# Splitting the first weight unit in two halves and reordering the first loads and the angle sums of an encoder kernel

## The chip, the cores and the metric
The kernel runs on one core of a Trainium2 chip. The metric is the device time of one execution in microseconds (us). The kernel before took 1182.69 us (median of three runs, 1182.65 to 1182.70). The engines are called PE (TensorE, matrix products), DVE (VectorE), ACT (ScalarE), POOL (GpSimd) and SP (the sync queue, which only issues transfers). POOL issues transfers too.

## The reference: what is computed
Two layers of an encoder on 512 tokens of width 1024. Each layer normalises x, modulates it by shift and scale (rows of c_act @ w_ada), multiplies it by the input weights w_in, and so on:

```python
c_act = jax.nn.silu(c)
mod = c_act @ w_ada[l] + b_ada[l]
sh1, sc1, g1, sh2, sc2, g2 = jnp.split(mod, 6, axis=-1)
h = modulate(rms_norm(x, norm1_g[l]), sh1, sc1)
z = h @ w_in[l]
za, zb, zq, zk, zv = jnp.split(z, split_idx, axis=-1)
...   # conformer convolution, short gated convolution, differential attention
x = x + g1[:, None, :] * mix
h = modulate(rms_norm(x, norm2_g[l]), sh2, sc2)
x = x + g2[:, None, :] * swiglu(h, w_gate_up[l], w_down[l])
```

The attention turns its queries and keys by cosines and sines of angles, positions times inverse frequencies (rope). These angles don't depend on x and are needed only after the first products.

## The kernel before, in words
Tokens lie along the free dimension: x is xT, 8 chunks (k = 0 to 7) of 128 features by 512 tokens. Every float32 product is made of three products of split operands (hi times hi, hi times lo, lo times hi). So each weight unit (a tile of 128 x 1024, 512 KB) lands in one of two `raw` slots, ACT copies it rounded into `w_hi` (`split_hi`, L676), and DVE subtracts to make `w_lo` (`split_lo`, L1108). SP loads unit u into slot u % 2 once `w_lo` of unit u - 2 is made (the loop at L512 to L515). `w_hi` and `w_lo` are rings of four.

**The first norm** is the place of the change. All of it is written out by hand, in program order on each engine:
- PE: three warm-up products, the spread of c over the partitions (L1916), 14 warm-up products of ones (`warm_up`, L1792, two records each in the trace), the sum of squares over the partitions (L1921, four products of 512 columns, two records each), 11 more warm-ups, and then for each chunk k an `a_chunk` (12 products, L1833, L1834, L1841: unit 0 for k = 0 and 1, unit 2 for k = 2 and 3, ...) and a `k_chunk` (12 products, L1851 to L1853: unit 1 for k = 0 and 1, unit 3 for k = 2 and 3, unit 5 for k = 4 and 5, unit 7 for 6 and 7). So 24 products stand for one chunk. An even chunk reads the first 512 columns of its unit and an odd chunk the second 512.
- ACT: silu of c, eight squares of x (L902), a table load, `split_hi(0)`, then rstd = exp(-0.5 ln(...)) in two steps (L745, L747) once the sum of squares is there, and `first_gain(0)` (L753, L755: the shift and gain of chunk 0). For each chunk: `norm_hi` (h_hi, L765), `split_hi(k + 1)`, `first_gain(k + 1)`. Behind it in chunk 3 a table load, in chunk 4 the three sines and a table load.
- DVE: the angles in turns (`angle_turns`, `sum_angles`: L1142, L1143 and the reduction L1144), four pair sums of the squares (L1138), `mod_dot(0)`, `mod_dot(1)` (L1161), `split_lo(0)`. Then for each chunk k: `norm_apply` (L1184, to work_b), one `mod_dot`, `norm_lo` (h_lo, L1192), another `mod_dot`, `split_lo(k + 1)`. In chunk 0 the order is apply, h_lo, mod_dot(2), split_lo(1), mod_dot(3). `reduce_angles` (L1148 to L1153, five small operations) stands behind chunk 1.
- `mod_dot(m)` is the product of silu(c) with block m of w_ada (512 KB, `ada_ring_first`). Blocks 2k and 2k + 1 are shift and scale of chunk k. POOL loads all sixteen (L540): 0 and 1 once the second quarter of x is there, 2 and 3 as 0 and 1 land, and block m from 4 on once DVE has finished m - 3 of them.

SP issues c, positions, frequencies, the four quarters of x, pcol (small per-feature constants), unit 0, and unit 1 once modulation block 0 has landed.

## Time and profile before
| | |
|---|---|
| median of three runs | 1182.69 us |
| the profiled execution | 1182.13 us, of which the span is 1180.3 us |
| PE busy | 99% of the span |
| DVE, ACT, POOL busy | 61%, 44%, 11% |

The span is what the profiler records from the first to the last instruction; 1.83 us of the execution lie around it. The times in rows are microseconds from the span's start. In a row of the timeline the columns are start, length, engine, line, operation, tiles, shapes, the count of merged records, and in brackets the engine's idle time before it with what ended it.

### The profile page before, as it was taken

To read this page: it belongs to the slowest core of one execution; us is meant where nothing else is said; L and a number is where in the kernel's file an instruction comes from. 1 tells how busy PE (TensorE), PEld (TensorE's weight loads), DVE (VectorE), ACT (ScalarE), POOL (GpSimd) and SP (SyncE) were. 2 spreads that over 40 slices of the span, in tenths; PEclk is the share of its full clock that TensorE was granted. 3 is DMA by queue.
4 is the path that set the end of the run, shared out by engine and by line. 5 is a ranking of instruction groups with operands and counts; after the bars stand their busy time and mean duration, and the time that the engine had idled before them with its cause. 6 is when DMAs were issued, how large, how long until landed. Compare 5 with 4: busy or idle time off the path is not lost.

```text
span 1180.3 us, 14480 instructions
## 1 busy us (share of the span) xinstructions
PE 1169.5 (99%) x5168; PEld 933.3 (79%) x5168; DVE 718.1 (61%) x1028; ACT 515.7 (44%) x782; POOL 125.0 (11%) x207
## 2 busy tenths in 40 slices
PE   9999999999999999999999999999999999999998
PEld 6787656878888888888888877578888888888887
DVE  7989888985555433577478988757633332333231
ACT  5576787452232323322234468866432222332220
POOL 2323233210102000121000112100000000000000
PEclk9999999999999999999999999999999999999999
DMA  8679477885655222697223663422322323233222
GB/s 307 246 179 252 79 188 227 301 277 191 198 192 178 89 96 99 233 323 252 101 91 104 162 143 72 108 71 91 124 90 93 102 89 107 89 104 101 102 105 87
DMA packets 50668, 178.32 MB, mean 151 GB/s; under 512 B 5889, under 2 KB 6017, under 8 KB 50626
## 3 DMA queue, kind: packets, MB, share of 16 engines
q1 hardware_dynamic: 30386, 107.13, 26.7%
q0 software_dynamic: 20240, 70.66, 21.8%
q8 instruction: 23, 0.38, 0.1%
q14 instruction: 19, 0.16, 0.0%
HBM read 172.52 MB, written 2.10 MB: 148 GB/s over the span
## 4 chain that ended last, share of the span: by engine, by line
PE 86%; DVE 8%; ACT 4%; issue 2%; DVEq 0%; ACTq 0%; POOL 0%; POOLq 0%
PE ps L1785 22%; PE ps L1786 22%; PE ps L1787 22%; PE ps L1814 3%; DVE uc L1296 2%; PE ps L1851 2%; PE ps L1853 2%; PE ps L1852 2%; PE ps L1818 2%; PE ps L2056 1%; PE ps L1908 1%; ACT prob L815 1%; PE ps L2031 1%; PE ps L1841 1%; PE ps L1833 1%
## 5 line engine op out<-in xcount | busy, mean ns | idle before, releaser
L676 ACT ACTIVATE w_hi<-raw 128x1024 fp32r<-128x1024 f32 x196 | 207.4, 1059 | 514.5 <-PE ps L1787 466.5
L1108 DVE TENSOR_TENSOR w_lo<-raw,w_hi 128x1024 fp32r<-128x1024 f32 x164 | 201.2, 1227 | 240.3 <-ACT w_hi L676 238.1
L1785 PE MATMUL ps<-h_hi,w_hi 128*128 128x512 f32 x832 | 331.5, 398 | 0.0
L1787 PE MATMUL ps<-h_lo,w_hi 128*128 128x512 f32 x832 | 324.2, 390 | 0.0
L1786 PE MATMUL ps<-h_hi,w_lo 128*128 128x512 f32 x832 | 324.1, 390 | 0.0
L1785 PEld LDWEIGHTS ps<-h_hi,w_hi 128*128 128x128 f32 x832 | 156.2, 188 | 43.4 <-issue 12.2
L1786 PEld LDWEIGHTS ps<-h_hi,w_lo 128*128 128x128 f32 x832 | 156.3, 188 | 34.0 <-issue 2.9
L1787 PEld LDWEIGHTS ps<-h_lo,w_hi 128*128 128x128 f32 x832 | 156.2, 188 | 32.7
L1786 PE MATMUL ps<-gu_hi,w_lo 128*128 128x512 f32 x352 | 137.0, 389 | 0.0
L1787 PE MATMUL ps<-gu_lo,w_hi 128*128 128x512 f32 x352 | 137.0, 389 | 0.0
L1785 PE MATMUL ps<-gu_hi,w_hi 128*128 128x512 f32 x352 | 137.0, 389 | 0.0
L1692 DVE TENSOR_TENSOR work_b<-ps,work_a 128x512 f32<-128x512 f32 x42 | 29.0, 691 | 110.0 <-PE ps L1787 86.6
L1787 PEld LDWEIGHTS ps<-gu_lo,w_hi 128*128 128x128 f32 x352 | 66.1, 188 | 13.7
L1785 PEld LDWEIGHTS ps<-gu_hi,w_hi 128*128 128x128 f32 x352 | 66.1, 188 | 13.7
L1786 PEld LDWEIGHTS ps<-gu_hi,w_lo 128*128 128x128 f32 x352 | 66.1, 188 | 13.7
L1851 PE MATMUL ps<-w_hi,h_hi 128*128 128x512 f32 x192 | 75.2, 392 | 0.2 <-DVE w_lo L1108 0.2
L1853 PE MATMUL ps<-w_hi,h_lo 128*128 128x512 f32 x192 | 74.8, 389 | 0.0
L1852 PE MATMUL ps<-w_lo,h_hi 128*128 128x512 f32 x192 | 74.8, 389 | 0.0
L1296 DVE SCALAR_TENSOR_TENSOR uc<-ua,pcol,uc 128x512 f32<-128x512 f32 x106 | 72.8, 743 | 0.0
L815 ACT ACTIVATE prob<-ps,neg_max 128x512 f32<-128x512 f32 x64 | 43.2, 682 | 16.8 <-DVE neg_max L1408 16.7
L1469 DVE SCALAR_TENSOR_TENSOR xT<-ps,mod,xT 128x512 f32<-128x512 f32 x31 | 23.2, 747 | 40.6 <-PE ps L1787 38.4
L1408 DVE TENSOR_REDUCE neg_max<-ps 128x2 f32<-128x1024 f32 x32 | 39.0, 1219 | 12.5 <-PE ps L2031 7.0
(229 smaller groups left out, 1408.6 us busy)
## 6 DMA issues: line engine op xcount, KB each, us to landing
raw<-w_stream SPq DMA_DIRECT2D x196, 512.0 KB, 3.3
w_lo<-w_stream POOLq DMA_DIRECT2D x32, 512.0 KB, 7.9
ada_ring_gu<-ada POOLq DMA_DIRECT2D x28, 512.0 KB, 4.2
ada_ring_late<-ada POOLq DMA_DIRECT2D x28, 512.0 KB, 5.4
ada_ring_first<-ada POOLq DMA_DIRECT2D x16, 512.0 KB, 5.0
ada_ring_mid_a<-ada POOLq DMA_DIRECT2D x12, 512.0 KB, 5.1
ada_ring_mid_b<-ada POOLq DMA_DIRECT2D x12, 512.0 KB, 6.0
tap_sum<-tap_product POOLq DMA_DIRECT2D x12, 256.0 KB, 7.2
```

The costliest lines, as they stand in the source:

```text
L676: act.activation(w_hi[:, u % RING, :], raw[:, u % RAW, :], ACT.Copy).then_inc(s_whi, 1)
L815: act.activation(prob[:, it % PROBS, comp, :], ps[:, 2 * (it % 2) + comp, :], ACT.Exp, bias=neg_max[:, it, comp:comp + 1], accum_out=row_s ...
L1108: dve.tensor_tensor(w_lo[:, u % RING, :], raw[:, u % RAW, :], w_hi[:, u % RING, :].bitcast(F32), ALU.subtract).then_inc(s_wlo, 1)
L1296: dve.scalar_tensor_tensor(uc[:, c, :], ua[:, c, j:j + T], w, uc[:, c, :], ALU.mult, ALU.add).then_inc(s_tap, 1)
L1408: dve.tensor_reduce(neg_max[:, it, :], ps[:, b:b + 2, :], AX_X, ALU.max, negate=True).then_inc(s_max, 1)
L1785: pe.matmul(dst, whi, rhs[0][:, n, :], start=start, stop=False)
L1786: pe.matmul(dst, wlo, rhs[0][:, n, :], start=False, stop=False)
L1787: return pe.matmul(dst, whi, rhs[1][:, n, :], start=False, stop=stop)
L1814: pe.matmul(ps[:, bank, :], wp[:, u % RING, n * P:(n + 1) * P], rhs[0][:, n, :], start=b == 0 and wp is w_hi, stop=False)
L1851: pe.matmul(ps[:, bank, :], hs[0], ws[0], start=n == 0, stop=False)
L1852: pe.matmul(ps[:, bank, :], hs[0], ws[1], start=False, stop=False)
L1853: return pe.matmul(ps[:, bank, :], hs[1], ws[0], start=False, stop=n == KC - 1)
```

## The change
It does the following, all in the first norm of the first layer:
- The sum of the angles (the reduction over nine terms) moves on DVE from ahead of the pair sums to behind chunk 3, `reduce_angles` from behind chunk 1 to behind chunk 4; on ACT the table load and the sines move one chunk later.
- Weight unit 0 lands, is copied and is subtracted in two halves of 512 columns. The first half's copy on ACT stands behind rstd instead of ahead of it; the second half's stands in chunk 0, and so does its subtraction on DVE, behind mod_dot(3).
- SP issues modulation blocks 1, 0, 2 and 3 in place of POOL; DVE takes block 1 before block 0. SP's loop over later units begins once the second half of unit 0 has its `w_lo`.
- PE has 9 warm-ups instead of 14 ahead of the sum of squares, and 18 instead of 11 behind it; its chunk 1 waits for the second half of unit 0.

```diff
@@ semaphores @@
+        s_rawpart = sem("second_half_first_unit_landed")
+        s_whipart = sem("second_half_first_unit_hi")
+        s_wlopart = sem("second_half_first_unit_lo")
+        s_adafirst = [sem(f"ada_first_landed{i}") for i in range(4)]
...
@@ sync queue @@
-            for j in range(RAW):
-                if j == 1:
-                    ada_landed(sp, 0)
-                sp.dma_start(raw[:, j, :], w_in[j]).then_inc(s_raw[j], 16)
+            sp.wait_ge(s_x[0], 16)
+            for m in (1, 0):
+                sp.dma_start(ada_slot(m), ada_in[m]).then_inc(s_adafirst[m], 16)
+            sp.dma_start(raw[:, 0, 0:T], w_in[0][:, 0:T]).then_inc(s_raw[0], 16)
+            ada_landed(sp, 1)
+            sp.dma_start(raw[:, 1, :], w_in[1]).then_inc(s_raw[1], 16)
+            sp.dma_start(ada_slot(2), ada_in[2]).then_inc(s_adafirst[2], 16)
+            sp.dma_start(raw[:, 0, T:UE], w_in[0][:, T:UE]).then_inc(s_rawpart, 16)
+            sp.dma_start(ada_slot(3), ada_in[3]).then_inc(s_adafirst[3], 16)
+            sp.wait_ge(s_wlopart, 1)
             begin = RAW
@@ GpSimd queue @@
-            pool.wait_ge(s_x[KC // 2 - 3], 16)
-            for m in range(2):
-                ada_load(m)
-            for m in range(2, 4):
+            for m in range(4, 6):
                 ada_landed(pool, m - 2)
                 ada_load(m)
-            for m in range(4, M_MID):
+            for m in range(6, M_MID):
                 pool.wait_ge(s_acc, m - 4 + 1)
                 ada_load(m)
@@ scalar engine @@
-            split_hi(0)
             norm_rstd(0)
+            act.wait_ge(s_raw[0], 16)
+            act.activation(w_hi[:, 0, 0:T], raw[:, 0, 0:T], ACT.Copy).then_inc(s_whi, 1)
             act.wait_ge(s_pc, 16)
...
+                        if k == 0:
+                            act.wait_ge(s_rawpart, 16)
+                            act.activation(w_hi[:, 0, T:UE], raw[:, 0, T:UE], ACT.Copy).then_inc(s_whipart, 1)
                         if k + 1 < KC:
                             first_gain(k + 1)
-                        if k == 3:
+                        if k == 4:
                             act.preload_act_table_set("silu_and_others")
-                        if k == 4:
+                        if k == 5:
                             act.wait_ge(s_ang, N_ANGLE)
@@ vector engine @@
-            def sum_angles():
+            def whole_turns():
 
                 done(dve.tensor_scalar(whole[:], turns[:], ROUND, None, ALU.add))
                 done(dve.scalar_tensor_tensor(turns[:], whole[:], ROUND, turns[:], ALU.subtract, ALU.subtract))
+
+            def sum_angles():
+
                 done(dve.tensor_reduce(ang[:, 0], turns[:], AX_X, ALU.add))
...
             angle_turns()
-            sum_angles()
+            whole_turns()
...
+            mod_dot(1)
             mod_dot(0)
-            mod_dot(1)
-            split_lo(0)
+            dve.wait_ge(s_whi, 1)
+            dve.tensor_tensor(w_lo[:, 0, 0:T], raw[:, 0, 0:T], w_hi[:, 0, 0:T].bitcast(F32),
+                              ALU.subtract).then_inc(s_wlo, 1)
...
+                        if k == 0:
+                            dve.wait_ge(s_whipart, 1)
+                            dve.tensor_tensor(w_lo[:, 0, T:UE], raw[:, 0, T:UE], w_hi[:, 0, T:UE].bitcast(F32),
+                                              ALU.subtract).then_inc(s_wlopart, 1)
                         if k:
                             split_lo(k + 1)
-                        if k == 1:
+                        if k == 3:
+                            sum_angles()
+                        if k == 4:
                             reduce_angles()
@@ tensor engine @@
                 weights_split(u)
+                if u == 0 and r:
+                    pe.wait_ge(s_wlopart, 1)
...
-            warm_up(N_WARM)
+            warm_up(N_WARM - 5)
...
-            warm_up(N_WARM - 3)
+            warm_up(N_WARM + 4)
```

DVE around the first chunk, before (L1144 is the angle reduction, L1138 the pair sums, L1161 the mod_dots, L1184 and L1192 the two operations of a norm chunk):

```order
L1144 TENSOR_REDUCE ang<-turns 128x128
L1138 TENSOR_TENSOR sq_first<-sq_first 128x512 x4
L1486 SCALAR_TENSOR_TENSOR n_biased<-pcol 128x8
L1161 SCALAR_TENSOR_TENSOR ada_ring_first,mod_raw<-ada_ring_first,c_b 128x1024 x2
L1108 TENSOR_TENSOR w_lo<-raw,w_hi 128x1024
L1184 SCALAR_TENSOR_TENSOR work_b<-xT,gain,rstd 128x512
L1192 SCALAR_TENSOR_TENSOR h_lo<-work_b,mod,h_hi 128x512
L1161 SCALAR_TENSOR_TENSOR ada_ring_first,mod_raw<-ada_ring_first,c_b 128x1024
L1108 TENSOR_TENSOR w_lo<-raw,w_hi 128x1024
L1161 SCALAR_TENSOR_TENSOR ada_ring_first,mod_raw<-ada_ring_first,c_b 128x1024
L1184 SCALAR_TENSOR_TENSOR work_b<-xT,gain,rstd 128x512
L1161 SCALAR_TENSOR_TENSOR ada_ring_first,mod_raw<-ada_ring_first,c_b 128x1024
```

and now (there the mod_dots are L1178, norm_apply L1201, norm_lo L1209, a whole `split_lo` L1122):

```order
L1152 TENSOR_TENSOR sq_first<-sq_first 128x512 x4
L1503 SCALAR_TENSOR_TENSOR n_biased<-pcol 128x8
L1178 SCALAR_TENSOR_TENSOR ada_ring_first,mod_raw<-ada_ring_first,c_b 128x1024 x2
L1509 TENSOR_TENSOR w_lo<-raw,w_hi 128x512
L1201 SCALAR_TENSOR_TENSOR work_b<-xT,gain,rstd 128x512
L1209 SCALAR_TENSOR_TENSOR h_lo<-work_b,mod,h_hi 128x512
L1178 SCALAR_TENSOR_TENSOR ada_ring_first,mod_raw<-ada_ring_first,c_b 128x1024
L1122 TENSOR_TENSOR w_lo<-raw,w_hi 128x1024
L1178 SCALAR_TENSOR_TENSOR ada_ring_first,mod_raw<-ada_ring_first,c_b 128x1024
L1529 TENSOR_TENSOR w_lo<-raw,w_hi 128x512
L1201 SCALAR_TENSOR_TENSOR work_b<-xT,gain,rstd 128x512
L1178 SCALAR_TENSOR_TENSOR ada_ring_first,mod_raw<-ada_ring_first,c_b 128x1024
```

The reduction has gone from ahead of the pair sums, `w_lo` of unit 0 is two operations of 512 columns, and the second of them stands between mod_dot(3) and the `norm_apply` of chunk 1.

SP from the quarters of x on, before, with what each waits for:

```order
L500 DMA xT<-x_t 128x1024 x4
L501 DMA pcol<-pcol 128x278
L505 DMA raw<-w_stream 128x1024
L505 DMA raw<-w_stream 128x1024 [waits ada_landed0]
L512 UNCONDITIONAL_BRANCH
L512 ISA
L515 ISA [waits weight_lo]
L515 DMA raw<-w_stream 128x1024
```

and now:

```order
L507 DMA xT<-x_t 128x1024 x4
L508 DMA pcol<-pcol 128x278
L511 DMA ada_ring_first<-ada 128x1024 [waits x_landed0]
L511 DMA ada_ring_first<-ada 128x1024
L512 DMA raw<-w_stream 128x512
L514 DMA raw<-w_stream 128x1024 [waits ada_first_landed1]
L515 DMA ada_ring_first<-ada 128x1024
L516 DMA raw<-w_stream 128x512
L517 DMA ada_ring_first<-ada 128x1024
L525 UNCONDITIONAL_BRANCH [waits second_half_first_unit_lo]
L525 ISA
L528 ISA [waits weight_lo]
L528 DMA raw<-w_stream 128x1024
```

Three modulation blocks and the halves of unit 0 have come in around unit 1 (`raw` 128x1024 at L514), a fourth block behind them, and the load of unit 2 (the first in the loop, L528) stands behind a wait for the second half's `w_lo`.

PE up to its first product of the layer, before and now:

```order
L1916 MATMUL ps<-c_row,ones 128x512 x2
L1792 MATMUL ps<-ones 128x128 x14
L1921 MATMUL ps<-sq_first,ones 128x512 x4
L1792 MATMUL ps<-ones 128x128 x11
L1833 MATMUL ps<-h_hi,w_hi 128x512
```

```order
L1943 MATMUL ps<-c_row,ones 128x512 x2
L1817 MATMUL ps<-ones 128x128 x9
L1948 MATMUL ps<-sq_first,ones 128x512 x4
L1817 MATMUL ps<-ones 128x128 x18
L1860 MATMUL ps<-h_hi,w_hi 128x512
```

The sum of squares stands five products earlier, and as many products and two more stand behind it.

## Rows read from the trace of the kernel before

**Rows 1.** The page, busy time by engine
```profile
PE 1169.5 (99%) x5168; PEld 933.3 (79%) x5168; DVE 718.1 (61%) x1028; ACT 515.7 (44%) x782; POOL 125.0 (11%) x207
```

**Rows 2.** Waits, 0 to 35 us: who for whom, us in total, times, longest
```profile
PE ps L1833 <- ACT h_hi L765: 2.0, 3, 1.2
```

**Rows 3.** Waits of PE, 35 to 110 us
```profile
PE ps L1851 <- DVE w_lo L1108: 0.2, 1, 0.2
```

**Rows 4.** Timeline of PE
```profile
6.35 6.10 PE L1792 MATMUL ps<-ones 128*128 128x128 f32 x28
12.29 3.60 PE L1921 MATMUL ps<-sq_first,ones 128*128 128x512 f32 x8
15.72 2.62 PE L1792 MATMUL ps<-ones 128*128 128x128 f32 x22
...
19.50 0.47 PE L1833 MATMUL ps<-h_hi,w_hi 128*128 128x512 f32 x1 [1.16 <-ACT h_hi L765]
...
35.29 0.50 PE L1851 MATMUL ps<-w_hi,h_hi 128*128 128x512 f32 x1 [0.24 <-DVE w_lo L1108]
...
46.32 0.39 PE L1851 MATMUL ps<-w_hi,h_hi 128*128 128x512 f32 x1
```

**Rows 5.** Timeline of DVE
```profile
9.41 1.35 DVE L1144 TENSOR_REDUCE ang<-turns 128x128 f32<-128x1152 f32 x1
10.80 2.50 DVE L1138 TENSOR_TENSOR sq_first<-sq_first 128x512 f32<-128x512 f32 x4
...
14.86 1.23 DVE L1161 SCALAR_TENSOR_TENSOR ada_ring_first<-ada_ring_first,c_b 128x1024 f32<-128x1024 f32 x1
...
16.01 1.22 DVE L1108 TENSOR_TENSOR w_lo<-raw,w_hi 128x1024 fp32r<-128x1024 f32 x1
17.85 0.75 DVE L1184 SCALAR_TENSOR_TENSOR work_b<-xT,gain,rstd 128x512 f32<-128x512 f32 x1 [0.62 <-ACT gain L755]
19.39 0.75 DVE L1192 SCALAR_TENSOR_TENSOR h_lo<-work_b,mod,h_hi 128x512 fp32r<-128x512 f32 x1 [0.79 <-ACT h_hi L765]
...
24.21 0.75 DVE L1184 SCALAR_TENSOR_TENSOR work_b<-xT,gain,rstd 128x512 f32<-128x512 f32 x1 [0.64 <-ACT gain L755]
...
28.96 0.22 DVE L1148 TENSOR_SCALAR ang<-ang 128x128 f32<-128x128 f32 x1
...
30.39 0.75 DVE L1184 SCALAR_TENSOR_TENSOR work_b<-xT,gain,rstd 128x512 f32<-128x512 f32 x1
...
34.02 1.22 DVE L1108 TENSOR_TENSOR w_lo<-raw,w_hi 128x1024 fp32r<-128x1024 f32 x1
35.15 0.74 DVE L1184 SCALAR_TENSOR_TENSOR work_b<-xT,gain,rstd 128x512 f32<-128x512 f32 x1
...
44.66 0.74 DVE L1184 SCALAR_TENSOR_TENSOR work_b<-xT,gain,rstd 128x512 f32<-128x512 f32 x1
```

**Rows 6.** Timeline of ACT
```profile
7.38 4.44 ACT L902 ACTIVATE sq_first<-xT 128x512 f32<-128x512 f32 x8
...
13.13 1.06 ACT L676 ACTIVATE w_hi<-raw 128x1024 fp32r<-128x1024 f32 x1
15.93 0.69 ACT L745 ACTIVATE rstd<-ps,eps 128x512 f32<-128x512 f32 x1 [1.74 <-PE ps L1921]
...
17.18 0.28 ACT L753 ACTIVATE mod<-mod_raw,pcol 128x1 f32<-128x1 f32 x1
...
43.64 0.30 ACT L753 ACTIVATE mod<-mod_raw,pcol 128x1 f32<-128x1 f32 x1 [1.19 <-DVE ada_ring_first L1161]
...
46.13 0.73 ACT L765 ACTIVATE h_hi<-work_b,mod 128x512 fp32r<-128x512 f32 x1
```

**Rows 7.** Tile raw, issue of unit 1 at 13.6 us: issue to landing
```profile
DMA to landing us min/median/max: 3.4/3.4/3.4
```

**Rows 8.** Tile raw, issue of unit 3 at 22.6 us: issue to landing
```profile
DMA to landing us min/median/max: 4.7/4.7/4.7
```

**Rows 9.** Tile raw, issue of unit 2 at 17.4 us: issue to landing
```profile
DMA to landing us min/median/max: 7.4/7.4/7.4
```

More of the change, by code:

```diff
@@ L478, in ada_landed @@
                 eng.wait_ge(s_ada_gu[m % 4], 16 * ((m - M_GU) // 4 + 1))
+            elif m < 4:
+                eng.wait_ge(s_adafirst[m], 16)
             else:
                 before = m // 8 if m < M_GU else M_GU // 8 + (m - M_DOWN) // 8
-                eng.wait_ge(s_ada[m % 8 if m < M_GU else (m - M_DOWN) % 8], 16 * (before + 1))
+                slot = m % 8 if m < M_GU else (m - M_DOWN) % 8
+                eng.wait_ge(s_ada[slot], 16 * (before + (slot >= 4)))
         def chunks_before(k):
```

## The prediction
> **What bounds the kernel now.** I read the page first: PE is busy for 1169.5 of 1180.3 us [rows 1], so the time is PE's work plus the little that PE waits. The waits by engine say where: up to 35 us PE waits 2.0 us in three pieces for h_hi [rows 2], and from 35 to 110 us only once, 0.2 us [rows 3]. PE's timeline puts that last wait at 35.29 us, where chunk 2's k_chunk starts as `w_lo` of unit 3 is made [rows 4]. From there PE runs back to back: from 35.29 to 46.32 us are two chunks, 5.5 us each, where DVE needs 4.75 (35.15 to 44.66 for two) [rows 4, 5]. So whatever moves the k_chunk at 35.29 moves the end by as much, and what comes onto DVE behind it is paid by its slack, if that is enough.
>
> The point at 35.29 hangs on DVE: the `norm_apply` of chunk 2 starts at 30.39, and everything between (two mod_dots, h_lo, `w_lo` of unit 3 at 34.02) is dense, 4.90 us to PE's start [rows 4, 5]. I call that operation apply(2) and follow it. The profiled execution took 1182.13 us, 1.83 more than its span, 0.56 less than the median of 1182.69. I take a difference of spans as the difference of times and put it on the median.
>
> **The angle reduction ahead of the pairs.** It takes 1.35 us and sits right ahead of the pair sums [rows 5]. Without it the pairs can start at 9.42 instead of 10.80, but the squares come at 0.555 us each until 11.82 [rows 6], so the fourth pair starts at 11.85 and ends at about 12.5 (0.68 each), against 13.3 before. Some 0.8 of the 1.35 is gained.
>
> **The sum of squares on PE.** Before, 14 warm-ups (28 records, 6.10 us, 0.212 us a step) held PE till 12.29, then the sum took 3.43 us until 15.72 [rows 4]. Now nine warm-ups end at 6.35 + 18 x 0.212 = 10.2 us. But the trace shows the two clock levels: a step of a 128-column record is 0.212 us before 12.29 and 2.62 / 22 = 0.119 behind 15.72, and a record of the sum, four times as wide, takes 0.43, twice the early step only [rows 4]. So PE ran at 1.2 GHz up to about 12.2 us, although it had been at work since before 6.35, and at 2.4 GHz behind it. If the clock rises at the same moment now, 1.95 us of the sum run at half speed and do 0.97 of its 3.43 us. It ends at 12.2 + 2.45 = 14.65 us, 1.07 earlier. If the clock were up already, it would end at 10.25 + 3.43 = 13.7, 2.0 earlier. If it rose only after the sum, it would end at 10.25 + 6.86 = 17.1, 1.4 later. I take 14.65: the records of the sum are no less dense than the warm-ups whose place they take.
>
> **rstd, the first half and the first apply.** rstd started 0.21 behind the end of the sum and its two steps took 1.25 until 17.18 [rows 6], so now 14.86 to 16.1. In front of the gain stands the copy of the first half, half of the 1.06 us of the whole [rows 6], 0.55; before, the whole copy lay in ACT's wait for the sum at 13.13. Gain at 16.65 to 17.2. DVE's half subtraction (0.65, by 1.22 for the whole [rows 5]) runs beside the gain, 16.65 to 17.3. So apply(0) starts at 17.3 instead of 17.85: 0.55 earlier. The mod_dots are done by then: pairs to 12.7, two at 1.15 each [rows 5] make 15.0, if block 1 has landed by 12.7 and block 0 by 13.9. SP issues them once the first quarter of x is there, which ACT's first square shows to be by 7.38 [rows 6]; POOL had waited for the second quarter, and both blocks were used from 14.86 at the latest [rows 5]. 1.6 us of room lie behind 15.0 before they would count. PE's 18 warm-ups take 36 x 0.117 = 4.2 us and end at about 18.9; h_hi comes to PE 1.65 us behind apply(0) [rows 4, 5], at 18.95, so they cost at most 0.1 there.
>
> **Chunk 0 to 1.** From apply(0) on DVE does h_lo (1.54 later), mod_dot(2), `w_lo` of unit 1, mod_dot(3), and now the second half of unit 0: 17.3 + 1.54 + 0.67 + 3 x 1.14 = 22.93 is its start, 23.6 its end [rows 5]. It fills the wait of 0.64 us for the gain [rows 5], so apply(1) starts at 23.66 instead of 24.21, the same 0.55. PE's chunk 1 starts 1.65 behind that, past the half. Blocks 2 and 3, unit 1 and the second half are issued as block 1 lands, by my reckoning near 11.5 us, where unit 1 had been issued at 13.6 [rows 7], and are needed at 18.8 or later; I cost them at nothing.
>
> **Unit 2, the step that decides.** Its slot is free when all of unit 0 has been subtracted: before at 17.23, now at 23.6. It was issued at 17.4 and had landed at 24.8 [rows 9], in time for a copy that has to follow h_hi of chunk 1, 0.8 us behind 24.21 [rows 5]. Now it is issued at 23.8. How long does it fly? Unit 1 took 3.4 us into nearly empty queues [rows 7]; unit 3, issued at 22.6 with one block a microsecond ahead and one behind it, 4.7 [rows 8]; the longest is 7.4, with four blocks in flight ahead [rows 9]. At 23.8 block 7 is issued half a microsecond ahead and most of the earlier ones are down, between the first two, so I take 4.1: landed at 27.9. Copy 1.1 us, `w_lo` of unit 2 1.14 us, apply(2) at 27.9 + 0.05 + 1.1 + 1.14 = 30.2. Without this wait it would be at 24.21 - 0.55 + (30.39 - 24.21) - 1.43 = 28.4, since `reduce_angles` (28.96 to 30.39) has left [rows 5]. So of the 2.0 us won by then, 1.8 are given back: DVE waits for ACT, ACT for unit 2, and behind ACT's waiting copy stands the gain of chunk 2. apply(2) is 0.2 us early, with 3.4 in place of 4.1 it is 0.9 early, with 4.7 0.4 late. The Trainium skill, DMA: Bandwidth & Descriptors, "Anatomy of one DMA", gives a fixed 2.0 us plus the bytes at 436 GB/s; for 512 KB that is 3.2 us, an estimate by that page under which apply(2) would be 1.1 early. No landing here of a unit beside modulation blocks is so short [rows 8, 9].
>
> **Behind the point.** Relative to the k_chunk of chunk 2, DVE now has 1.37 (reduction) and 1.43 (`reduce_angles`) more. Its gain on PE is 0.7 us a chunk. Stepping through: unit 5's `w_lo` comes 0.16 before PE wants it, h_hi of chunk 5 0.1 late, h_hi of chunk 6 no later (ACT's gain to h_hi takes 2.49 with the sines between [rows 6], which now stand there), unit 7's `w_lo` another 0.2 late. I put 0.25 us for it, between 0 (PE ahead of nothing) and 0.6. Behind chunk 7 DVE has room and the angle tables are needed late.
>
> **Sum.** -0.2 + 0.25 = +0.05 us: 1182.69 + 0.05, no change, 1182.7 us.
>
> **The rivals.**
> (a) Unit 2 lands faster or the clock is up earlier. With 3.4 us in flight: -0.9 + 0.25 = -0.65. With the sum all at 2.4 GHz the whole start is 0.9 earlier: -1.1 at 4.1 us and -1.8 at 3.4, with 0.25 back -0.85 and -1.55. For it: the queues are emptier than at 22.6. Against: 0.212 us a step until 12.2 [rows 4]. Time 1181.6.
> (b) Slower: the sum of squares meets the low clock to its end. It decides if PE has not risen to 2.4 GHz by 17.1 us. Then rstd is 2.45 later than in my sum, nothing on DVE catches it up, and apply(2) is 2.25 late; with 0.25 behind it +2.5, 1185.2 us. For it: the five warm-ups taken away stood just where the clock rose. Against: the sum is as dense, and three runs before agree within 0.05 us, so the moment looks fixed. The Trainium skill, TensorE: Matmul & The Clock Gate, Part 1, says the moment depends on the run ("the same kernel measures 6, 11, or 14 cold-MMs"); by that the runs would scatter between (a) and (b). The trace does not agree so far.
> (c) Slower by the queue: unit 2 takes as long as it did before, 7.4 us, behind blocks 6 and 7. apply(2) is at 33.5, +3.1, with 0.25 +3.35: 1186.0 us.
> (d) Something of the 2.0 us kept that I give back (no wait for unit 2 at all): -2.0 + 0.25, 1180.9 us at most, with the high clock 1180.0.
>
> **How the numbers follow.** Forecast 0.50 (its own range 1182.0 to 1183.6), (a) 0.30, (b) 0.07, (c) 0.06, (d) 0.07. A difference under 0.2% (2.4 us) can't be told from no change in this kernel. Forecast, (a) and half of (d) lie inside it, (b) at its edge, (c) past it: faster 0.04, same 0.86, slower 0.10. The range for eight in ten holds the forecast and (a): 1181.1 to 1184.1.
>
> **What would show it.** Sum of squares ending at 14.6 to 14.7, its first two records twice as long as the last. apply(0) at 17.3, apply(1) at 23.7. SP's issue of unit 2 at 23.8 in place of 17.4, and ACT's copy of unit 2 idle for it for 2 to 3 us, which rows of before do not have. apply(2) near 30.2, k_chunk 2 near 35.1, and then short waits of PE for h_hi of chunk 5 and `w_lo` of unit 7. I am wrong if ACT has unit 2 at hand when it comes to it, if PE's sum ends past 16, or if PE idles more than half a microsecond behind 36 us.

## The result: 3.3 us slower, where no change was forecast
The changed kernel took 1185.6 us (median of nine runs, 1184.32 to 1187.29), the kernel before beside it 1182.33 (nine runs, 1181.59 to 1184.48). The ratio is 1.0027, its 95% interval 1.0018 to 1.0035: slower by 3.3 us, outside the forecast's range of 1181.1 to 1184.1. The ratios with their intervals are those on record; where a kernel has only five to nine runs they can differ from the quotient of the two medians by up to 0.0008, which is 0.9 us. The profiled execution took 1185.41 us with a span of 1183.6, 3.3 more than before's.

In this part lines are those of the changed kernel: 1817 is the warm-up, 1948 the sum of squares, 1860 the first product of an `a_chunk`, 1878 that of a `k_chunk`; on DVE 1201 is `norm_apply`, 1209 h_lo, 1178 mod_dot, 1122 `split_lo`, 1509 and 1529 the two halves of unit 0, 1161 the reduction; on ACT 686 is `split_hi`, 755 rstd, 775 h_hi, 917 the first half's copy.

The page's first row reads as it did [rows 1]: PE's share doesn't show 3 us, since waits of that size are 0.3% of the span.

```profile
PE 1170.7 (99%) x5172; PEld 932.4 (79%) x5172; DVE 718.8 (61%) x1029; ACT 515.6 (44%) x783; POOL 122.9 (10%) x203
```

PE's timeline of the changed kernel, against [rows 4]:

```profile
6.36 4.21 PE L1817 MATMUL ps<-ones 128*128 128x128 f32 x18
10.36 4.02 PE L1948 MATMUL ps<-sq_first,ones 128*128 128x512 f32 x8
14.22 4.18 PE L1817 MATMUL ps<-ones 128*128 128x128 f32 x36
18.64 0.47 PE L1860 MATMUL ps<-h_hi,w_hi 128*128 128x512 f32 x1 [0.24 <-ACT h_hi L775]
...
32.59 0.47 PE L1860 MATMUL ps<-h_hi,w_hi 128*128 128x512 f32 x1 [1.87 <-ACT h_hi L775]
...
35.84 0.50 PE L1878 MATMUL ps<-w_hi,h_hi 128*128 128x512 f32 x1 [0.24 <-DVE w_lo L1122]
...
58.91 0.50 PE L1878 MATMUL ps<-w_hi,h_hi 128*128 128x512 f32 x1 [0.81 <-DVE w_lo L1122]
...
101.12 0.50 PE L1878 MATMUL ps<-w_hi,h_hi 128*128 128x512 f32 x1 [0.87 <-DMA w_lo<-w_stream]
```

The start is as forecast: chunk 0 begins at 18.64 in place of 19.50. Then stand three waits that before has not, or has shorter: 1.87 us for h_hi of chunk 2, 0.81 for `w_lo` of unit 7, 0.87 for a weight unit near 100 us. DVE's and ACT's timelines say what the first one hangs on [rows 5, 6]; DVE's is this:

```profile
9.28 2.04 DVE L1152 TENSOR_TENSOR sq_first<-sq_first 128x512 f32<-128x512 f32 x3
...
16.38 0.69 DVE L1509 TENSOR_TENSOR w_lo<-raw,w_hi 128x512 fp32r<-128x512 f32 x1 [1.65 <-ACT w_hi L917]
16.99 0.75 DVE L1201 SCALAR_TENSOR_TENSOR work_b<-xT,gain,rstd 128x512 f32<-128x512 f32 x1
...
22.62 0.69 DVE L1529 TENSOR_TENSOR w_lo<-raw,w_hi 128x512 fp32r<-128x512 f32 x1
23.35 0.75 DVE L1201 SCALAR_TENSOR_TENSOR work_b<-xT,gain,rstd 128x512 f32<-128x512 f32 x1
...
29.81 1.23 DVE L1122 TENSOR_TENSOR w_lo<-raw,w_hi 128x1024 fp32r<-128x1024 f32 x1 [2.75 <-ACT w_hi L686]
30.95 0.74 DVE L1201 SCALAR_TENSOR_TENSOR work_b<-xT,gain,rstd 128x512 f32<-128x512 f32 x1
...
40.46 1.34 DVE L1161 TENSOR_REDUCE ang<-turns 128x128 f32<-128x1152 f32 x1
...
51.63 1.22 DVE L1122 TENSOR_TENSOR w_lo<-raw,w_hi 128x1024 fp32r<-128x1024 f32 x1
...
55.97 1.48 DVE L1178 SCALAR_TENSOR_TENSOR ada_ring_first<-ada_ring_first,c_b 128x1024 f32<-128x1024 f32 x1
...
57.38 1.47 DVE L1122 TENSOR_TENSOR w_lo<-raw,w_hi 128x1024 fp32r<-128x1024 f32 x1
```

ACT's, with its long wait for unit 2:

```profile
14.48 0.69 ACT L755 ACTIVATE rstd<-ps,eps 128x512 f32<-128x512 f32 x1 [1.54 <-PE ps L1948]
...
28.72 1.06 ACT L686 ACTIVATE w_hi<-raw 128x1024 fp32r<-128x1024 f32 x1 [3.85 <-DMA raw<-w_stream]
```

SP's timeline has the issue of units 2 and 3 (two transfers in one row), and the tile `raw` says for unit 2 how long it flew, in us from issue to landing, where [rows 9] had 7.4 for it, hidden:

```profile
23.66 0.89 SPq L528 DMA_DIRECT2D raw<-w_stream  x2
```

```profile
DMA to landing us min/median/max: 5.0/5.0/5.0
```

The chain reads: the second half of unit 0 is subtracted by 23.3, SP issues unit 2 at 23.66, it lands 5.0 us later, ACT copies at 28.72, DVE subtracts at 29.81 and applies chunk 2 at 30.95, which was at 30.39 before.

Three marks cut the difference into parts: the `k_chunk` of chunk 2, that of chunk 7, and the first transpose of k, in us from the span's start. Behind the last mark the rest of the span is 1074.0 to 1074.6 in all sixteen profiles, so all but a few tenths of a microsecond of the difference arises in the first 110 us.

| profile | k_chunk 2 | k_chunk 7 | transpose | span |
|---|---|---|---|---|
| before | 35.29 | 62.64 | 106.20 | 1180.3 |
| changed | 35.84 | 64.52 | 109.42 | 1183.6 |
| added in the part | +0.55 | +1.33 | +1.34 | +0.1 |

Up to the last mark that is 3.2 us, and 3.3 in the span.

### The profile page after: what moved, and what is told of

The parts are those of the page before. It is cut to its first block, busy times and chain, and to the rows that moved or that the text cites. A ratio compares the mean times of both kernels' runs of the same rounds, so it can differ in the third digit from the quotient of the medians.

```text
span 1183.6 us, 14491 instructions
## 1 busy us (share of the span) xinstructions
PE 1170.7 (99%) x5172; PEld 932.4 (79%) x5172; DVE 718.8 (61%) x1029; ACT 515.6 (44%) x783; POOL 122.9 (10%) x203
## 4 chain that ended last, share of the span: by engine, by line
PE 79%; DVE 8%; ACT 4%; DMA 2%; issue 2%; POOL 0%; DVEq 0%; ACTq 0%; SPq 0%; POOLq 0%
PE ps L1810 22%; PE ps L1812 22%; PE ps L1811 22%; PE ps L1839 3%; DVE uc L1313 2%; PE ps L1843 2%; PE ps L2083 1%; PE ps L1935 1%; ACT prob L825 1%; PE ps L2058 1%; DMA tap_sum<-tap_product 1%; DVE w_lo L1122 1%; PE ps L2071 1%; DMA w_lo<-w_stream 1%; PE ps L2052 1%
## 5 line engine op out<-in xcount | busy, mean ns | idle before, releaser
L1122 DVE TENSOR_TENSOR w_lo<-raw,w_hi 128x1024 fp32r<-128x1024 f32 x163 | 200.0, 1227 | 243.3 <-ACT w_hi L686 240.8
L1810 PEld LDWEIGHTS ps<-h_hi,w_hi 128*128 128x128 f32 x832 | 156.2, 188 | 43.2 <-issue 12.2
L1810 PEld LDWEIGHTS ps<-gu_hi,w_hi 128*128 128x128 f32 x352 | 66.1, 188 | 13.7
L1812 PEld LDWEIGHTS ps<-gu_lo,w_hi 128*128 128x128 f32 x352 | 66.1, 188 | 13.7
```

Source lines behind the costliest of these rows:

```text
L1122: dve.tensor_tensor(w_lo[:, u % RING, :], raw[:, u % RAW, :], w_hi[:, u % RING, :].bitcast(F32), ALU.subtract).then_inc(s_wlo, 1)
L1810: pe.matmul(dst, whi, rhs[0][:, n, :], start=start, stop=False)
L1812: return pe.matmul(dst, whi, rhs[1][:, n, :], start=False, stop=stop)
```

## The experiments
The theory from the two traces: (T) unit 2's late issue and its flight set chunk 2, and the angle work comes due at unit 7. The rivals: (R1) the angle move alone costs the time; (R2) the moved clock rise; (R3) the wait near 100 us is the change's doing.

**Which part costs.** The first is the kernel before with the angle moves alone.

```diff
-            sum_angles()
+            whole_turns()
@@ DVE, chunks (on ACT the table load and the sines move one chunk later too) @@
-                        if k == 1:
+                        if k == 3:
+                            sum_angles()
+                        if k == 4:
                             reduce_angles()
```

> The kernel before with only the angle sums moved (reduction behind chunk 3, reduce_angles behind chunk 4, table load and sines one chunk later on ACT). Theory 1 (the loss of the change comes from the late load of unit 2, and the angle work behind chunk 3 is mostly within DVE's slack): the k_chunk of chunk 2 starts 1.4 us earlier than before (33.9 us), 0.3 to 1.1 us are given back by short waits of PE in chunks 5 to 7, the time is 0.3 to 1.1 us below before. Rival (the moved angle work is what costs, since DVE has no room there): 0.5 us or more above before.

Measured: 1182.87 us against 1182.80, ratio 0.9999 (0.999 to 1.0008). R1 falls: it asked for 0.5 us or more above before. But the gain of 0.3 to 1.1 us that I expected isn't there either. The early part of it is, `k_chunk` 2 at 34.03, 1.3 us earlier than before, and it is given back in two waits, for unit 7 and for the unit near 100 us. PE's timeline of it:

```profile
56.62 0.50 PE L1856 MATMUL ps<-w_hi,h_hi 128*128 128x512 f32 x1 [0.57 <-DVE w_lo L1108]
...
98.59 0.50 PE L1856 MATMUL ps<-w_hi,h_hi 128*128 128x512 f32 x1 [0.75 <-DMA w_lo<-w_stream]
```

The second is the changed kernel with the angle work put back where it stood before.

```diff
             whole_turns()
+            sum_angles()
@@ DVE, chunks (on ACT the table load and the sines move back too) @@
-                        if k == 3:
-                            sum_angles()
-                        if k == 4:
+                        if k == 1:
                             reduce_angles()
```

> The changed kernel with the angle work back in its old places: only the loads, the halves and the warm-ups are changed. Theory 1: the pair sums are 1.3 us later again, unit 2 still lands late (near 29.3 us) and reduce_angles again stands between its w_lo and the norm_apply of chunk 2, so the k_chunk of chunk 2 starts near 38.0 us, 2.7 later than before; nothing is late behind it: 2.5 to 3.5 us above before. Rival (the angle work costs, the loads do not): within 0.5 us of before.

Measured: 1188.65 us, ratio 1.0053 (1.0039 to 1.0066), 5.85 us slower, so the loads cost more than the whole change does, and the angle moves take some of it back. It is over 2 us more than I expected (2.5 to 3.5, with `k_chunk` 2 near 38.0). The pair sums are late again here, so the sum of squares ends only at 15.5. Unit 2 was issued at 24.92 and flew 6.3 us. ACT and PE of this kernel:

```profile
31.29 1.06 ACT L686 ACTIVATE w_hi<-raw 128x1024 fp32r<-128x1024 f32 x1 [5.17 <-DMA raw<-w_stream]
```

```profile
36.60 0.51 PE L1859 MATMUL ps<-h_hi,w_hi 128*128 128x512 f32 x1 [4.62 <-ACT h_hi L775]
```

Its granted clock reads 0.95 in 36 to 37 us and 0.50 (the 1.2 GHz level) in each of the next three: a cost that the prediction had not priced. `k_chunk` 2 came at 41.01.

**Take the late issue away.** The changed kernel, in which the second half of unit 0 is copied right behind h_hi of chunk 0 and subtracted right behind its h_lo.

```diff
+                        if k == 0:
+                            act.wait_ge(s_rawpart, 16)
+                            act.activation(w_hi[:, 0, T:UE], raw[:, 0, T:UE], ACT.Copy).then_inc(s_whipart, 1)
                         if k < RING - 1:
                             split_hi(k + 1)
@@ DVE, chunk 0 @@
                         if k == 0:
+                            dve.wait_ge(s_whipart, 1)
+                            dve.tensor_tensor(w_lo[:, 0, T:UE], raw[:, 0, T:UE], w_hi[:, 0, T:UE].bitcast(F32),
+                                              ALU.subtract).then_inc(s_wlopart, 1)
                             mod_dot(2)
                             split_lo(1)
```

> The changed kernel with the second half of unit 0 copied on ACT ahead of unit 1 and subtracted on DVE ahead of mod_dot(2), so that SP issues unit 2 about 2.4 us earlier. Theory 1 (unit 2 decides): issued near 21.2, landed by 26.5, no wait of DVE for its copy; norm_apply of chunk 1 0.6 later (24.0), that of chunk 2 at 28.8 instead of 30.95, the k_chunk of chunk 2 at 33.7, 2.1 us less than the changed kernel if the waits behind stay. Rival (the loss sits behind chunk 4 and in the accumulating loads near 100 us and would come out whatever the start): less than 0.7 us gained.

Measured: 1183.24 us, ratio 1.0002 (0.9993 to 1.0011). Unit 2 is issued at 20.58; it flies 5.8 us, longer than in the first profile of the changed kernel, but ACT waits only 0.59 for it and `k_chunk` 2 is at 34.22. Of 3.3 us lost, 2.8 are back (0.44 us above before in place of 3.3) by an edit that leaves every operation and every transfer as it was and brings only the second half's copy and subtraction, and with them the issue of unit 2, three microseconds forward. This is the strongest evidence for T. It does not tell apart what the edit saves by the usual flight and what by the long ones that come up below.

**Lighten the queues.** In the next kernel the late issue stays, but POOL holds blocks 7, 8 and 9 until unit 2 has landed.

```diff
             for m in range(6, M_MID):
+                if m == 7:
+                    pool.wait_ge(s_raw[0], 32)
                 pool.wait_ge(s_acc, m - 4 + 1)
```

> The changed kernel in which GpSimd holds modulation block 7 back until unit 2 has landed, so that unit 2, issued at the same 23.7 us, meets only block 6. In three profiles of the changed kernel's first part its flight was 5.0, 7.0 and 7.1 us. Theory (its flight beside modulation blocks is the mis-sized term and the source of the spread, and flights of 7 us also let PE's clock fall): flight 3.2 to 4.2 us, k_chunk of chunk 2 at 34.3 to 35.2, granted clock 1.00 throughout, median 1.0 to 2.5 us below the changed kernel beside it, spread under 2.5 us. Rival (the flight is long whatever is beside it, or the loss is made good elsewhere): flight over 4.8 us or median within 0.5 us.

> The changed kernel once more as the control beside e13: median 2 to 3.5 us above before, flight of unit 2 between 5 and 7.1 us; where PE waits for it over 3 us the granted clock falls to 0.50 for 2 to 5 us behind.

Measured on the same chip: 1183.92 us (ratio 1.001, 1.0001 to 1.0019) with the hold, 1185.66 (1.0028, 1.0018 to 1.0038) for the changed kernel as it is. The hold gains 1.74 us, and its runs spread over 2.2 us in place of 5. The flight only fell from 5.0 to 4.7, not to the 3.2 to 4.2 expected, and without any hold it was 4.6 in one profile of a variant (tables late, below): these profiles don't show that blocks 7 and 8 lengthen the flight. What is left beside unit 2 in the kernel with the hold is unit 3, issued right behind it; that unit 3 makes the rest of the 4.7 is argued, no run here moves it. In the two profiles `k_chunk` 2 differs by 0.67 (35.01 and 35.68), and 0.38 of this stands already in the issue of unit 2 (23.16 and 23.54), since the sum of squares ended earlier in the one with the hold. So the gain of the median is more than the profiles show; the next run says why it can be.

**The changed kernel again, and PE's warm-ups.**

> The changed kernel once more, on the chip of the three runs beside it, with a second profile. Same places as in its first profile: unit 2 issued near 23.7 us, k_chunk of chunk 2 near 35.8, w_lo of unit 7 late for the k_chunk of chunk 6, an added unit late near 101 us. 2.1 to 4.0 us above before. The moment at which PE's clock rises (11.2 us in the first profile, 9.5 to 12.2 in the others) may be another, and moves the end of the sum of squares by half as much.

```diff
-            warm_up(N_WARM - 5)
+            warm_up(N_WARM)
@@ behind the sum @@
-            warm_up(N_WARM + 4)
+            warm_up(N_WARM - 3)
```

> The changed kernel with the warm-ups as before (14 ahead of the sum of squares, 11 behind), so that the sum starts at 12.3 us, at the high clock in any run. Theory: it ends at 15.7 instead of 14.2, everything up to the k_chunk of chunk 2 is 1.4 us later (37.2), the wait for unit 7 is the same, 1.0 to 1.6 us above the changed kernel in the median, and the times of single runs spread less (the changed kernel's: 3.0 us). Rival (the spread comes from the transfers): the spread stays. Second rival (the early sum brings nothing since unit 2 waits for DMA anyway): within 0.4 us of the changed kernel.

Measured: the changed kernel 1185.3 us, ratio 1.0021 (1.0011 to 1.0032); with 14 warm-ups ahead of the sum 1187.61 (five runs), ratio 1.0036 (1.0022 to 1.0049). That is 2.3 us above the changed kernel where I expected 1.0 to 1.6, and the spread stays (4.75 us). Keeping the old warm-ups doesn't help, so taking them away is not in itself the cause. Over the three profiles of the changed kernel the sum took 4.02, 4.71 and 3.90 us and always ended by 14.9, against 15.7 before. So a late clock rise costs nothing directly against before. That doesn't clear R2 as the trigger of a long flight, as the table below shows.

The profile of the changed kernel in this series fell on one of its long executions (1187.81 us), and shows what the medians hold. PE, then ACT:

```profile
10.36 4.71 PE L1948 MATMUL ps<-sq_first,ones 128*128 128x512 f32 x8
...
35.23 0.47 PE L1860 MATMUL ps<-h_hi,w_hi 128*128 128x512 f32 x1 [3.82 <-ACT h_hi L775]
```

```profile
31.35 1.06 ACT L686 ACTIVATE w_hi<-raw 128x1024 fp32r<-128x1024 f32 x1 [5.81 <-DMA raw<-w_stream]
```

Unit 2, issued at 24.34, flew 7.0 us. The windows of this execution, a microsecond each (columns: width, busy time of PE, PEld, DVE, ACT, POOL with counts, granted clock, busy share of the DMA engines, GB/s):

```profile
36.00:37.00 1.00, 1.00 (x5) 0.82 (x4) 1.00 (x2) 0.04 (x1) 0.30 (x1) 0.74 0.51 201
37.00:38.00 1.00, 1.00 (x4) 0.81 (x3) 1.00 (x3) 0.57 (x2) 0.42 (x1) 0.50 0.92 315
38.00:39.00 1.00, 1.00 (x4) 0.71 (x4) 1.00 (x2) 0.00 (x0) 0.10 (x1) 0.50 0.70 250
39.00:40.00 1.00, 1.00 (x4) 0.80 (x3) 1.00 (x2) 0.88 (x2) 0.00 (x0) 0.56 0.87 279
40.00:41.00 1.00, 1.00 (x6) 0.81 (x5) 1.00 (x4) 0.79 (x1) 0.48 (x1) 1.00 0.68 242
```

After 3.82 us of idle time PE fell to 1.2 GHz from 36.5 to about 39.9. From the last a_chunk's start to its k_chunk were 4.18 us where the first profile had 3.25: 0.9 us more. With 1.87 us of idle time the clock had stayed at 1.00. Why 7.0 and not 5.0? The stretch 24 to 31 us of the changed kernel's first profile, and then of this one:

```profile
24.00:31.00 7.00, 6.36 (x27) 4.62 (x25) 4.25 (x8) 2.24 (x4) 1.06 (x2) 1.00 0.98 387
```

```profile
24.00:31.00 7.00, 6.63 (x29) 5.18 (x28) 3.70 (x6) 0.72 (x1) 1.27 (x3) 1.00 0.86 290
```

The first moved 387 GB/s at a busy share of 0.98, the second 290 at 0.86: not more bytes in the queue but slower ones. What slows them no run here shows. But the eight profiles in which unit 2 waits for the second half behind mod_dot(3) fall into two groups (us; the last column is over all runs of the kernel, its clock is explained next):

| profile | sum of squares ends | unit 2 issued | its flight | PE then idle | runs with a mean clock below 1.000 |
|---|---|---|---|---|---|
| blocks 7 to 9 held | 13.7 | 23.16 | 4.7 | 1.58 | 1 of 11 |
| changed, third | 14.1 | 23.54 | 5.0 | 1.87 | 11 of 26, all three series |
| changed, thin tap sums (below) | 14.1 | 23.56 | 5.4 | 2.22 | 7 of 11 |
| changed, first | 14.2 | 23.66 | 5.0 | 1.87 | as above |
| changed, tables late (below) | 14.3 | 23.71 | 4.6 | 1.45 | 4 of 5 |
| changed, again | 14.9 | 24.34 | 7.0 | 3.82 | as above |
| 14 warm-ups ahead | 15.2 | 24.59 | 7.1 | 3.94 | 4 of 5 |
| loads only | 15.5 | 24.92 | 6.3 | 4.62 | 5 of 5 |

All five issued by 23.71 flew at most 5.4 us, all three issued from 24.34 on at least 6.3, and the two kernels whose edit makes the start late (14 warm-ups ahead, loads only) dip in nine of ten runs. In the changed kernel the one late start came from a late clock rise. So an issue 0.6 us or more later and a long flight go together here; that the one brings the other is not shown, and no run moves the start alone. With it the run with 14 warm-ups can't decide on R2: it took the uncertain clock rise away, but put the issue among the late ones.

Runs without a profile list only their mean granted clock, but that speaks too. It was 1.000 in all 97 timed runs of the kernel before that stood beside the experiments. In the 26 of the changed kernel it was below 1.000 in 11, whose median is 1185.87 against 1185.3 of the other 15; in 5 of 5 with the loads alone, in 1 of 11 with blocks 7 to 9 held, in none of 11 with the half early. A mean of 0.999 can also come from a dip at the very end (one profile further down has it there, at no cost), so this is a hint and not a count. Nor does this clock show everything: in the windows from 6 to 14 us it reads 1.00 in the profiles of the kernel before and of the changed kernel, though a record of the warm-ups takes 0.21 to 0.22 us up to 10.36, the step of the lower speed, and 0.12 behind the sum. The hint fits that the hold above saves the long flights more than it shortens the usual one.

**The wait at unit 7.** DVE's operations of 1.22 us take 1.47 at 56 to 59 us. POOL makes the rope tables then:

```profile
53.77 1.74 POOL L608 TENSOR_TENSOR tabs<-trig,rows 128x128 f32<-128x128 f32 x2
55.46 2.31 POOL L611 TENSOR_TENSOR tabs<-trig,rows 128x128 f32<-128x128 f32 x2
57.73 2.30 POOL L608 TENSOR_TENSOR tabs<-trig,rows 128x128 f32<-128x128 f32 x2
```

The next kernel makes POOL wait for the last chunk's h before the tables.

```diff
             pool.wait_ge(s_trig, 3)
+            pool.wait_ge(s_h, KC)
             rope_tables(0)
```

> The changed kernel in which GpSimd's eight angle table products wait until DVE has done h_lo of chunk 7. In the changed kernel they ran from 53.8 to 60.9 us, beside DVE operations that took 1.47 instead of 1.22 us, the last of them w_lo of unit 7, for which PE waited 0.81 us. Theory (the two engines slow each other there): these DVE operations take 1.22 again, the wait falls to 0.2 to 0.4 us, 0.5 to 0.6 us less than the changed kernel. Rival (DVE is late by its own work): same wait, same time.

Measured: 1186.77 us (five runs, 1184.4 to 1188.91), ratio 1.0041 (1.0027 to 1.0055). In its profile unit 7's subtraction takes 1.22 again, and PE's wait for it is gone:

```profile
56.47 1.22 DVE L1123 TENSOR_TENSOR w_lo<-raw,w_hi 128x1024 fp32r<-128x1024 f32 x1
```

`k_chunk` 7 is at 63.33 against 64.52, 0.8 of it behind `k_chunk` 2. But the median did not follow, it is the higher one. Four of the five runs have a mean clock below 1.000, so long flights may have covered the gain; that is not shown. To see the tables without that, they were moved in the kernel with the half early (both edits above together).

> e4 (second half of unit 0 early) and e3 (GpSimd's tables behind chunk 7) together. Theory (both mend a part): k_chunk of chunk 2 near 34.1, no wait of more than 0.3 us for w_lo of unit 7, 0.4 to 0.8 us below e4, at or below before. Rival (the tables only move the conflict to the taps and the added units, as e3's median of 1186.8 suggests): above e4.

Measured: 1182.34 against 1182.46, ratio 0.9997 (0.9988 to 1.0006), and no wait for unit 7 in its profile. Against its own kernel before it is 0.56 better than the half early alone was. That is the size of the 0.60 us wait that it removes, but the intervals of both are wider than this.

**The wait near 100 us.** The unit that is waited for there is loaded by POOL with tap sums ahead of it. In the next two kernels the tap sums move 64 of their 512 columns, in the changed kernel and in the kernel before; both leave the convolution's sums incomplete and serve for the time alone.

```diff
-                    pool.dma_start(tap_sum[:, c, :], tap_product[:, (r - CC) % TAP_SLOTS, :],
+                    pool.dma_start(tap_sum[:, c, 0:64], tap_product[:, (r - CC) % TAP_SLOTS, 0:64],
```

> The changed kernel in which GpSimd's adding transfers of the tap products carry 64 of 512 columns (an eighth of the bytes; the convolution's sums are left incomplete). Theory (the third part of the loss is PE waiting at 101 us for an added w_lo that comes late, because SP's units, GpSimd's added units and the tap sums fill the DMA engines from 72 to 112 us, and the stretch starts late): the wait of 0.87 us at 101 us goes, the rest stays (k_chunk of chunk 2 near 35.8, 0.8 us for w_lo of unit 7): 1.0 to 1.4 us below the changed kernel, about 1.5 to 2.2 above before. Rival (that wait comes of GpSimd's or ACT's program order, not of the bytes): it stays.

> The kernel before with the same thin tap transfers (the convolution's sums are left incomplete), as the control of the run above. It has no such wait, so within 0.3 us of before. If it gains as much as the changed kernel does, the third part is no part of the change.

Measured: 1184.9 us (ratio 1.002, 1.0011 to 1.0029) changed, 1181.86 (0.9994, 0.9985 to 1.0003) before. The wait is gone from the profile of the changed kernel, and the last part of the table shrinks to the 43.5 us that it has before. But the kernel before has a median 0.6 lower as well (I had expected at most 0.3, and its interval holds no gain too), and the difference of the two stays 3.0 us. So R3 is no large part of the loss: the wait comes with those transfers, 1.5 us in one execution and nothing in another. Of the +1.34 in the table little is the change's in the medians. None at all is not shown: the only two profiles of the kernel before (one with thin taps) have no such wait, and all three of the changed kernel have it (0.87, 0.82, 0.77).

**Versions made to beat both.** The first is the kernel before with the angle moves taken further: the reduction behind chunk 5, `reduce_angles` behind chunk 7, on ACT the table load behind chunk 6 and the sines not in the chunks but behind the copy of unit 9. Its edit is shown against the first experiment's kernel.

```diff
-                        if k == 3:
+                        if k == 5:
                             sum_angles()
-                        if k == 4:
+                        if k == 7:
                             reduce_angles()
@@ ACT @@
+                    if l == 0 and s == A_AT[l][-1]:
+                        act.wait_ge(s_ang, N_ANGLE)
+                        ...   # the three sines, from chunk 5
```

> The kernel before with the angle work moved as in e1, but later: the reduction behind chunk 5, reduce_angles behind chunk 7, the sines behind ACT's copy of unit 9. Theory (DVE's lateness behind chunk 4 is what gave e1's gain back, by w_lo of unit 7 and by the late start of the loads behind it): k_chunk of chunk 2 at 33.9 us, no wait in chunks 5 to 7, waits for added units below 0.4 us, 0.9 to 1.4 us below before. Rival (from 72 to 112 us the DMA engines set the time whatever the start): PE waits 1 us more for added units, within 0.4 us of before.

Measured: 1181.31 us, ratio 0.999 (0.9981 to 0.9999): 1.15 us below before and 4 below the changed kernel, the lowest median of all. `k_chunk` 2 is at 33.81 and `k_chunk` 7 at 61.01, 27.2 us behind it, without a wait. Only the wait near 100 us is left:

```profile
97.71 0.50 PE L1856 MATMUL ps<-w_hi,h_hi 128*128 128x512 f32 x1 [0.77 <-DMA w_lo<-w_stream]
```

The second puts the same angle order into the changed kernel and hides the halves: the first half's copy ahead of rstd, the second half issued right behind the first and subtracted between apply and h_lo of chunk 0; it has 15 warm-ups behind the sum in place of 18. The third is that with 14 and 11 warm-ups.

```diff
+            act.wait_ge(s_raw[0], 16)
+            act.activation(w_hi[:, 0, 0:T], raw[:, 0, 0:T], ACT.Copy).then_inc(s_whi, 1)
             norm_rstd(0)
-            act.wait_ge(s_raw[0], 16)
-            act.activation(w_hi[:, 0, 0:T], raw[:, 0, 0:T], ACT.Copy).then_inc(s_whi, 1)
...
             sp.dma_start(raw[:, 0, 0:T], w_in[0][:, 0:T]).then_inc(s_raw[0], 16)
+            sp.dma_start(raw[:, 0, T:UE], w_in[0][:, T:UE]).then_inc(s_rawpart, 16)
             ada_landed(sp, 1)
```

> A version meant to beat both: the changed kernel with the angle work as in e7, the first half's copy on ACT back ahead of rstd (lands near 13.9 us, rstd starts at 14.5), the second half issued right behind the first, copied behind the first gain and subtracted between norm_apply and h_lo of chunk 0, where DVE waits 0.79 us for ACT; 15 instead of 18 warm-ups. Theory: norm_apply of chunk 0 at 16.4, unit 2 issued near 17.8, norm_apply of chunk 2 near 27.6, k_chunk of chunk 2 near 32.5; 1.5 to 2.7 us below before. Rival (DMA stretch): within 0.5 us of before.

> The version of e8 with the warm-ups as before. Theory: the sum ends at 15.7 instead of 14.0, but norm_apply of chunk 1 and 2 had waited for modulation blocks in e8 too, so that only part of 1 us is lost: 0.3 to 1.0 us above e8, equal to e7 within 0.5 us, with less spread than e8's 3.6 us. Rival: the spread stays.

Measured: 1181.97 us (0.9996, 0.9987 to 1.0005) and 1182.29 (0.9997, 0.9988 to 1.0006). Unit 2 is issued at 18.51 in the first and hidden. I had expected `k_chunk` 2 near 32.5 and 1.5 to 2.7 us below before; it came at 33.96, and the time is 0.5 below, as the rival had it. What the split had won is partly lost again in DVE's timeline, where mod_dot(2) waits 0.36 us and the mod_dot between apply and h_lo of chunk 1 0.57 us for their blocks to land. Its profile has the shortest span of all, 1179.0, but its runs spread over 3.6 us and the median is not below that of the angles alone. So in these versions splitting unit 0 is worth nothing that can be measured, even with unit 2 hidden; one in which the blocks also land in time was not run.

## Why the prediction was wrong, step by step
- **The start came out right, in part by luck.** Forecast and measured: warm-ups' end 10.2 and 10.36, end of the sum 14.65 and 14.22, apply(0) 17.3 and 16.99, second half's subtraction done and apply(1) 23.66 and 23.35, issue of unit 2 23.8 and 23.66. The sum took 3.90 to 4.71 us in the three profiles: it takes 3.60 when all of it runs at the upper speed, so by my estimate from these lengths the clock rose near 11.2 us in the first and near 12.6 in the longest, and not at a fixed 12.2. I had called the moment fixed because three runs of before agreed; but before's sum starts at 12.29, behind it, and so could not show it. The Trainium skill, TensorE: Matmul & The Clock Gate, "What's actually happening", says that the number of slow matmuls at the start varies from run to run; the three profiles of the changed kernel agree with it. It moves the start by 0.8 us between these three (unit 2 was issued at 24.34, 23.66 and 23.54), and the late one is the one with the long flight.
- **The first term that failed: 4.1 us for unit 2's flight.** It flew 5.0, 7.0 and 5.0 us in the three profiles. That I bounded it by 3.4 and 4.7 was the error: the row of 4.7 is for a queue with one block a microsecond ahead [rows 8], and I read 23.8 us as emptier, though block 7 and, half a microsecond behind it, unit 3 share the engines, which moved 387 GB/s without a gap. Which of them makes the difference is open: with blocks 7 to 9 held it still flew 4.7. In none of the sixteen profiles did unit 2 fly less than 4.2 us, so the 3.2 us of the prediction met no case. With 5.0 my own steps give: landed at 28.7, apply(2) at 30.9; it was at 30.95. In the usual execution this term is worth 0.75 us (+0.55 at apply(2) in place of -0.2). Rival (c), with 7.4, is the same mechanism at its other end; I gave it 0.06, and one profile in three of the changed kernel has it.
- **The cost behind a long flight was not in any rival.** A flight of 6.3 to 7.1 us leaves PE idle for 3.8 to 4.6 us, and then the granted clock falls to 0.50 (1.2 GHz), for 3.4 us in two profiles and 6.8 in the third. In the profile with 7.0, `k_chunk` 2 is 4.1 us late, where (c) has 3.1.
- **The second term that failed: the 0.25 us behind the point.** It is off by more than the first, 1.1 us in the profile. Both places were named right, h_hi of chunk 5 and `w_lo` of unit 7. The sizes were 0.2 and 1.0, the latter against 0.2: 1.33 us by the marks in place of 0.25. I counted the 2.8 us of angle work, but took DVE's durations from a stretch without neighbours. Beside POOL's tables its operations take 1.47 for 1.22, with the tables late 1.22 again, and there the part behind `k_chunk` 2 is 0.8 us shorter; the other 0.5 of the 1.33 is left for the angle work. The two engines slow each other: POOL's table products take 0.45 us each where DVE leaves them alone (seven of the eight in the best kernel), and up to 1.44 here. Before shows the same slowing in DVE's timeline, at the same moment, with 2.93 us of room behind it, and I had left it out of the sum:

```profile
57.35 1.37 DVE L1108 TENSOR_TENSOR w_lo<-raw,w_hi 128x1024 fp32r<-128x1024 f32 x1
...
63.47 1.29 DVE L1280 TENSOR_TENSOR ua<-ps,uc 128x512 f32<-128x512 f32 x2 [2.93 <-ACT uc L777]
```

  The Trainium skill, SBUF — State Buffer, "Who interferes with whom", says that a DVE instruction with two SBUF inputs contends with a GpSimd instruction that reads SBUF. The rows agree, for `w_lo` and mod_dot alike; by that rule it could have been forecast that there is a term at unit 7, though not its 0.25 us an operation.
- **A term that stood at nothing: the wait near 100 us.** The prediction ended its sum at chunk 7. The three profiles of the changed kernel have 0.8 to 0.9 us there, and 1.1 to 1.3 up to the transpose; by the thin taps little of it is the change's in the medians.
- **The sum as it should stand** for the usual execution: apply(2) +0.55, behind it +1.33 less what a later start hides, together 1.9 us; and in an execution with a 7 us flight +4.1 and little behind it (`k_chunk` 7 at +4.4, since DVE catches up). The medians' +2.8 to +3.3 in the three series lie between. But the sum doesn't close: the 15 runs whose clock reads 1.000 should be the usual ones, and their median still lies 2.6 us above that of before beside them, 0.7 more than 1.9. A share in the wait near 100 us could fill this; it stays open. How often each kind of execution comes can't be read from runs without a profile, so the split of the median is argued, while that the early issue gives most of it back (2.8 of 3.3 us) is shown.
- **"Wrong if PE idles more than half a microsecond behind 36 us"**: it does, 0.81 and 0.87. The first is the change's; the second is by the thin taps for the most part not, though neither profile of the kernel before has it.

Open stay why unit 2's transfer is slow in some executions and whether a late start brings it, how much of the hold's 1.74 us comes from such executions, and why the late tables alone had a higher median (1186.77, five runs) than the changed kernel itself, though their profile is the better one.

## What to carry to other kernels
Splitting a load so that its first half is used earlier frees its slot later: find who is issued into that slot, and price that flight by a row with as many transfers beside it, up to the longest in the trace (7.4 us here, against 7.0 met), not by a quieter one. When work is moved into an engine's slack, take the durations from the stretch that it moves to, and its neighbours with them. A long wait of PE can cost its own length and the clock behind it (0.9 us more behind one of 3.8 us, nothing behind one of 1.9), so the price of a late transfer is not a straight line. And what has no reader soon, as the angle work, goes as late as it can: moved further than the change does, alone, it gave the lowest median of the study, 1.15 us below before.

## What the hardware showed unexpectedly
- Transfers of 512 KB took 4.6 to 7.1 us between issue and landing at the same place of nearly the same program (387 GB/s in all in a profile with 5.0 us, 290 in one with 7.0), the long ones where unit 2 was issued 0.6 us or more later; the execution is steady elsewhere (span behind the first transpose equal within 0.6 us).
- PE's granted clock stayed at 1.00 behind idle times of up to 2.2 us, and fell to 0.50 for 3.4 to 6.8 us around or behind 3.8 to 4.6. By the windows it fell before PE had resumed with 3.94 us of idle time, and 1.3 and 0.3 us after with 3.82 and 4.62. From 6 to 10 us the row reads 1.00 while PE's steps are the long ones, 0.21 to 0.22 us a warm-up record against 0.12 later.
- DVE's two-input operations of 1.22 us take 1.47 beside POOL's table products, 20% more, while single products of POOL go from 0.45 to up to 1.44 us, so POOL can lose 1 us in an operation where DVE loses 0.25.
